# HGRN and gated linear attention: copy the last token tiles first, round the next weights after the first unit's exponentials

## The reference

```python
def chunk_gla(q, k, v, g):
    # S_t = diag(exp(g_t)) S_(t-1) + k_t v_t^T ; o_t = S_t^T q_t, a decay per key channel
    G = jnp.cumsum(g, axis=-2)
    def step(S, inp):
        q_c, k_c, v_c, G_c, qd_c, kd_c, gl_c = inp
        rel = jnp.exp(jnp.where(incl, G_c[..., :, None, :] - G_c[..., None, :, :], -jnp.inf))
        a = jnp.einsum('bhcd,bhsd,bhcsd->bhcs', q_c, k_c, rel)
        o_c = jnp.einsum('bhcd,bhde->bhce', qd_c, S) + jnp.einsum('bhcs,bhse->bhce', a, v_c)
        ...

def hgrn2(x, w_in, lb, norm_w, w_out):
    q, f, i, r = jnp.split(x @ w_in, 4, axis=-1)     # gates from f, values from i
    ...
    o = chunk_gla(q, k, i, log_f)                    # 8 heads of 128; GLA: 4 heads
    o = gated_rms_norm(o, r, norm_w)
    return o @ w_out
```

## Time and profile before

| | |
|---|---|
| median of 3 runs | 2507.51 us (2505.46 to 2508.47) |
| profiled execution | 2507.87 us, of which the span of the trace is 2506.2 |
| PE busy | 2430.0 us, 97% of the span |
| DVE, ACT, POOL busy | 71%, 47%, 4% |
| mean granted TensorE clock | 0.985 of full speed |
| HGRN, last token product to last score in place | 1474 to 1523 us |
| GLA, the same | 1828 to 1859 us |

### The profile page before, as it was taken

One profiled execution on the slowest core, in us unless ns is written; L12 is line 12 of the kernel. 1 busy time (PEld: TensorE's weight loads), 2 busy tenths in 40 slices (PEclk: granted clock), 3 DMA queues, 4 the chain that ended last, 5 costly groups with the idle time before them and its releaser, 6 DMA issues.

```text
span 2506.2 us, 47998 instructions
## 1 busy us (share of the span) xinstructions
PE 2430.0 (97%) x18262; PEld 2248.3 (90%) x18262; DVE 1767.6 (71%) x2908; ACT 1187.6 (47%) x1849; POOL 108.3 (4%) x161
## 2 busy tenths in 40 slices
PE   9999999999999999989999999999989999989998
PEld 6867977788898999988999998999989999978998
DVE  5878799988847866685665867666467657676665
ACT  5554522223645444465444545444545446465444
POOL 2221000000000000000300000000000000000000
PEclk9999999999999999999999999999999999999999
DMA  7423355554424555322555532555424554322554
GB/s 301 143 101 135 110 184 188 181 183 157 177 93 144 195 178 164 118 93 68 180 185 190 162 107 68 192 181 181 160 67 162 185 174 161 102 86 76 195 176 132
DMA packets 119709, 378.21 MB, mean 151 GB/s; under 512 B 11655, under 2 KB 29063, under 8 KB 119184
## 3 DMA queue, kind: packets, MB, share of 16 engines
q1 hardware_dynamic: 107040, 328.62, 39.3%
q0 software_dynamic: 12528, 47.62, 5.6%
HBM read 375.15 MB, written 1.05 MB: 150 GB/s over the span
## 4 chain that ended last, share of the span: by engine, by line
PE 83%; DVE 10%; ACT 4%; issue 2%; DMA 1%; SPq 0%; DVEq 0%; ACTq 0%
PE gb L643 22%; PE gb L644 21%; PE gb L645 21%; DVE w_lo L612 2%; PE mb L2996 2%; PE mb L751 1%; ACT w_hi L604 1%; PE mb L644 1%; PE mb L643 1%; PE mb L645 1%; PE gb L2977 1%; DMA X<-in_x 1%; DVE W L2731 1%; DVE R L1620 1%; DVE W L1620 1%
## 5 line engine op out<-in xcount | busy, mean ns | idle before, releaser
L643 PE MATMUL gb<-Xs,w_hi 128*128 128x256 f32 (+1 forms) x3454 | 1053.6, 305 | 17.8 <-DVE w_lo L612 5.8
L645 PE MATMUL gb<-Xs,w_lo 128*128 128x256 f32 (+1 forms) x3454 | 1036.4, 300 | 0.0
L644 PE MATMUL gb<-Xs,w_hi 128*128 128x256 f32 (+1 forms) x3368 | 1007.7, 299 | 0.0
L604 ACT ACTIVATE w_hi<-raw 128x1024 fp32r<-128x1024 f32 x586 | 614.9, 1057 | 733.6 <-PE gb L645 681.5
L612 DVE TENSOR_TENSOR w_lo<-raw,w_hi 128x1024 fp32r<-128x1024 f32 x586 | 709.6, 1222 | 217.6 <-ACT w_hi L604 211.1
L643 PEld LDWEIGHTS gb<-Xs,w_hi 128*128 128x128 f32 x3454 | 655.5, 190 | 67.6 <-issue 25.0
L645 PEld LDWEIGHTS gb<-Xs,w_lo 128*128 128x128 f32 x3454 | 655.6, 190 | 26.8
L644 PEld LDWEIGHTS gb<-Xs,w_hi 128*128 128x128 f32 x3368 | 639.9, 190 | 23.6 <-issue 1.7
L644 PE MATMUL gb<-Fs,w_hi 128*128 128x256 f32 (+1 forms) x966 | 277.2, 287 | 0.0
L643 PE MATMUL gb<-Fs,w_hi 128*128 128x256 f32 (+1 forms) x880 | 247.7, 281 | 0.0
L645 PE MATMUL gb<-Fs,w_lo 128*128 128x256 f32 (+1 forms) x880 | 246.1, 280 | 0.0
(11 more groups left out here) (459 smaller groups left out, 3315.7 us busy)
## 6 DMA issues: line engine op xcount, KB each, us to landing
raw<-in_up SPq DMA_DIRECT2D x264, 512.0 KB, 3.3
raw<-in_down SPq DMA_DIRECT2D x96, 512.0 KB, 3.7
R<-in_mod_later POOLq DMA_DIRECT2D x80, 512.0 KB, 3.9
raw<-in_gdn_in SPq DMA_DIRECT2D x64, 512.0 KB, 3.3
raw<-in_down SPq DMA_DIRECT2D x48, 384.0 KB, 3.9
raw<-in_hgrn_in SPq DMA_DIRECT2D x32, 512.0 KB, 4.4
raw<-in_ev_in SPq DMA_DIRECT2D x24, 512.0 KB, 5.2
raw<-in_gla_in SPq DMA_DIRECT2D x24, 512.0 KB, 3.9
```

The lines of the kernel that those rows point to most:

```text
L604: nc.scalar.activation(hi, raw[:, slot, 0:hi.shape[1]] if len(hi.shape) == 3 else like(raw[:, slot], hi), ACT.Identity).then_inc(*hi_ready ...
L643: nc.tensor.matmul(to, weight_block(w_slot, 0, k), x_hi, start=start, stop=False)
L644: nc.tensor.matmul(to, weight_block(w_slot, 0, k), x_lo, start=False, stop=False)
L645: return nc.tensor.matmul(to, weight_block(w_slot, 1, k), x_hi, start=False, stop=stop)
```

## The change

A new function `act_last_tokens` takes the place of `act_keep_tokens` in the second pass of token tiles, in HGRN and in GLA. It rounds two tiles (0' and 1') after the first pair as before, makes the first two copies, and then makes the other two copies with no rounding ahead of them. The roundings of 2' and 3' are in `act_gla_core`, behind the exponentials of unit 0. DVE makes three rests instead of four in that pass, and the rest of 2' behind the last `place`, ahead of the normalisation. The loops of one trip around the pass are gone on ACT and DVE. PE, SP and POOL have the same instructions as before.

```diff
--- before.py
+++ after.py
@@ -3041,6 +3041,9 @@
                     nc.scalar.activation(span_exp[u % 2][:, :, 4 * b:4 * b + 4, :],
                                          gb[:, 2 * b:2 * b + 2, :].rearrange("p c (t l i) -> p l (c t) i", t=2, l=2), ACT.Exp,
                                          scale=1.0 / 16 if z.name == "gla" else 1.0).then_inc(*spans_exp.inc())
+                if u == 0:
+                    for _ in range(2):
+                        split_hi(act, ahead["act"].next())
             level_rows.due("act", 4)
 
             def square(c):
@@ -3099,9 +3102,19 @@
                 if u + 1 < len(z.units):
                     rows(u + 1)
                 place(u)
+            dve_tile(dve)
             head_out.due("dve", 4)
             gn_dve_out(dve, z.items, z.parts)
 
+
+        def act_last_tokens(act, to):
+
+            act_tile(act, 2, wait=True)
+            for u in range(BANKS):
+                if u >= 2:
+                    act.wait_ge(*gemm_out.due("act"))
+                gemm_taken.due("act")
+                nc.scalar.activation(to[u // 2][:, u % 2:u % 2 + 1, :], gb[:, u, 0:T].unsqueeze(1), ACT.Identity).then_inc(*gemm_taken.inc())
 
         def pe_hgrn(pe, ready):
             z = hgrn_
@@ -3134,7 +3147,7 @@
             act.wait_ge(*gate_turned.due("act"))
             for b in range(4):
                 nc.scalar.activation(Xs[:, 2 * b:2 * b + 2, T:2 * T], score_banks[b].rearrange("p (a c) -> p a c", a=2), ACT.Identity).then_inc(*gate_hi.inc())
-            act_keep_tokens(act, 4, T, lambda i: z.v[:, :, bass.ds((i + 2) * T, T)])
+            act_last_tokens(act, [z.v[:, :, 2 * T:3 * T], z.v[:, :, 3 * T:4 * T]])
             act_gla_core(act, z)
 
         def dve_hgrn(dve):
@@ -3184,7 +3197,9 @@
                 last = nc.vector.tensor_tensor(Xs[:, KC + 2 * b:KC + 2 * b + 2, T:2 * T], score_banks[b].rearrange("p (a c) -> p a c", a=2),
                                                Xs[:, rows, T:2 * T], ALU.subtract)
             last.then_inc(*gate_lo.inc())
-            dve_pass(dve, 4)
+            dve_tile(dve, 3)
+            gemm_out.due("dve", 4)
+            gemm_taken.due("dve", 4)
             dve_gla_core(dve, z)
 
 
```

## The result

| | before | after |
|---|---|---|
| median of the runs of one occasion | 2504.86 us (20 runs, 2499.84 to 2511.44) | 2500.90 us (20 runs, 2496.50 to 2506.22) |
| profiled execution, its span | 2507.87, 2506.2 us | 2500.57, 2498.9 us |
| mean granted clock | 0.985 | 0.987 |

The ratio is 0.9980, with a 95% interval of 0.9973 to 0.9987: the changed kernel is 5.0 us faster by the ratio (3.3 to 6.8), and 4.0 by the two medians. The forecast was 4.6 us less (2502.9 against 2507.51, 0.9982) and most likely no difference of over 0.2% (0.54). Two executions on record, one of before at 7695.36 us and the profiled one of long_fill at 11646.79 us, stand apart from all others and are used in no ratio and no reading.

The account below looks back on a forecast made before the run. PE was taken as the bound, busy 2430.0 of 2506.2 us, so only its idle waits pay. From the median 2507.51, less 3.82 for the copies and 0.8 for the clock, other terms 0: 2502.9 us, range 2500.4 to 2506.0.

Parts of the forecast that it names:

- Term 1: PE's wait before exponents(0) in HGRN and GLA: copies start 1.91 us earlier in each, 3.82 us gained in all.
- Term 2: ACT between exponentials of units 0 and 1: moved roundings cost PE 0; 1.59 us idle left in HGRN, GLA 0.19 late.
- Term 3: DVE ahead of the normalisation L1391: the moved rest of 2' takes 1.16 of 2.36 us idle, cost 0.
- Term 4: SP's load of tile 6' into slot 2: issued later but landing 9 us before ACT's rounding, cost 0.
- Term 5: PE's clock at the two 2.72 us gaps: a quarter of a fall at each, 0.8 us gained, ends 0 and 3.0.
- The class: Whole kernel, borders at 0.2% (5.0 us) from no change: within 0.54, faster 0.43, slower 0.03.
- B: Clock falls usual at one of the two gaps are gone: 2500.7 to 2502.1 us, middle 2501.3; chance 0.43.
- C: Half the gain: the wait returns in HGRN or GLA as another one, 2505.6 us; chance 0.05.
- D: ACT loads tables twice per layer around the moved roundings, 3.7 us late together, 2507.4 us, no gain; chance 0.01.
- E: Moved work not covered: roundings delay unit 1's exponentials, the rest of 2' delays normalisation, 2509.8 us; chance 0.03.
- F: Clock falls three times in HGRN's units of 64-column scores, 3.0 us each, 2512.7 us, slower; chance 0.03.

Follow-up runs that it names:

- long_fill: long_gap with six unused 512-column products on PE in each of the two gaps: 2511.45 us against 2506.51 for the kernel before, ratio 1.0014.
- hgrn_only: The whole change in HGRN alone, GLA as in the kernel before: 2503.56 us against 2506.87, ratio 0.9989.
- gla_only: The whole change in GLA alone, HGRN as in the kernel before: 2503.42 us against 2506.87, ratio 0.9986.
- dve_only: Kernel before with only DVE's part (three rests in the pass, the rest of 2' behind the last place), ACT unchanged: 2508.40 us against 2506.87, ratio 1.0008.
- long_gap: Kernel before with the two roundings ahead of the last copies each made twice in both mixers: 2513.44 us against 2505.66, ratio 1.0033.
- long_fill_look: The same kernel as long_fill, run once more for its profile: 2508.27 us (one run) against 2508.28 for the kernel before.
- fill_short: Kernel before with three unused 512-column products on PE in each 2.72 us gap: 2506.86 us against 2506.51, ratio 1.0004.
- hi_before_exp: Changed kernel with the two roundings behind the copies but ahead of unit 0's exponentials: 2502.74 us against 2506.87 for the kernel before, ratio 0.9983.

## Why the prediction was right, and where it failed

**Term 1, the copies go ahead: right.** 2 x 1.91 were forecast and 2 x 1.97 measured, and the gap is 0.75 instead of 0.81. HGRN's core is 1.94 shorter, so what follows moves along whole; hgrn_only and gla_only show each alone.

**Term 2, the roundings on ACT at 0: right.** 1.61 us remain in HGRN. In GLA the second exponentials start directly behind the roundings and PE doesn't wait for them: exponents(2) has no idle time ahead of it. Counted from exponents(0) they start 0.09 us later than before, where 0.19 was forecast.

**Term 3, the rest of 2' at 0: right.** 1.22 us in DVE's idle time, 1.23 left (forecast 1.2), and dve_only shows the cores unchanged.

**Term 4, the load of 6' at 0: right by the profile.** The rounding of 6' stands here in the timeline of ACT in the kernel after:

```profile
1539.53 1.04 ACT L604 ACTIVATE Rr<-raw 128x1024 fp32r<-128x1024 f32 x1
```

It starts 62.23 us behind PE's last token product (1477.30), and before it was 64.16 (1537.84 less 1473.68): 1.93 earlier, as all the rest. SP issues the load of 6' at 1526.14, the DMA engines are busy for the next two rows (the last two numbers are their share and GB/s) and idle in the third, so it is there by about 1530, 9.5 us ahead of the rounding (forecast 9):

```profile
1526.00:1528.00 2.00, 2.00 (x13) 1.74 (x12) 0.75 (x1) 0.72 (x2) 0.00 (x0) 1.00 0.46 117
1528.00:1530.00 2.00, 2.00 (x11) 1.55 (x10) 0.75 (x1) 1.70 (x3) 0.00 (x0) 1.00 0.36 145
1530.00:1532.00 2.00, 2.00 (x11) 1.42 (x10) 1.35 (x2) 1.70 (x4) 0.00 (x0) 1.00 0.00 0
```

No run took this step alone.

**Term 5, the clock at 0.8: its size is not settled, and its reason was wrong.** The gains of the change (4.0 to 5.0 on the first occasion, 4.8 to 4.9 on the second) leave 0 to 1 us beside the waits' 3.9, and the estimate from the mean granted clocks is 2.2 us (0.2 to 4.2); 0.8 is inside both. The prediction placed the falls at the gaps of 2.72 us; no profile of any kernel has one there, in 8 gaps of 2.72. They come at 4.89, and behind the wait of 1.17. In the two profiled executions the fall made 3.15 of 7.3 us, near the 3.0 of the prediction's estimate of one fall. That one of the two had it is the luck of the moment at which scores(0) came, by the raster above.

The Trainium skill's "TensorE: Matmul & The Clock Gate", section "What's actually happening", was quoted as a rule by which less idle time can only help. long_gap against long_fill_look agrees (half clock behind 4.89 us of idle time, full clock with PE busy in it); the median of fill_short, 0.04% above before, shows nothing of it. Its section "A second HAM failure mode: psum-queue depth-cycling" describes short, frequent idle times between groups of products by which the clock falls and rises again; here a single wait of 1.17 us was enough, so the case is like it in the shortness and not in the frequency.

**The class: this is the step that failed.** The prediction held 0.2%, 5.0 us, to be what a measurement can tell from no change. It gave no reason for this number, and from it put the likeliest case, a gain of 4.6 us, on the side of no difference, with 0.54. The measured ratio had an interval of 0.07% on each side, 1.7 us, and 4.6 us is 2.6 times that. The gain was forecast to within 0.6 us of what came, by the ratio or by the medians; the border was wrong, not the sum. A second part is the reference: 2507.51 is a median of three, and executions of this kernel lie between 2499.84 and 2511.44, so a median of three can be 2 or 3 us off. That alone moved the forecast time from 2500.3 (2504.86 less 4.6) to 2502.9, against 2500.90 measured, which is only 0.5 above the low end of the range.

**The rivals.** B (the clock gives more, 2501.3) has the time, and by luck: the 2.65 us of the reference put 2500.90 on its side of the border. Its mechanism, a usual fall at one of the two gaps, is in none of the 8 gaps of 2.72; a share of the clock by another way, the moment of scores(0), is not excluded. C is refuted by both gaps being 0.75; D by the missing table load; E by hi_before_exp too, in which the roundings are in the worse place and cost 0.5 us; F by HGRN's core, which has no stretch at half clock.

## What to carry to other kernels

When two things wait in an in-order queue, put first what releases the bounding engine, and look for independent work on that engine for what is left of the wait: here reordering the copies gave about 4 us, and PE's own scores put into the wait gave 2.6 us more of the cores' length. Give the size of a gain as the forecast, and take the border of "no difference" from the spread and number of runs: with 20 runs that spread over 0.5%, 0.1% could be told. Compare stage lengths between fixed points of two traces before reading anything from their spans, since one fall of the clock in one of two profiles (3.15 us) is nearly as large as the effect.

## What the runs showed of the hardware

- Behind idle times of PE of 2.72 us the granted clock stayed full in 8 of 8 places; behind 4.89 us it was 0.50 in 2 of 2; behind 4.9 us in which PE made filler products it was full in 2 of 2.
- A wait of only 1.17 us was followed by 6.83 us at 0.50 in GLA in 7 of 12 profiles, at the products of 64 columns. One such fall costs 3.15 us. Making PE busy in the gap ahead (long_fill_look) didn't prevent it. The moment of scores(0) against the execution's own changes of the clock separates the 7 from the 5, and with the wait filled or cut to 0.21 us none of 3 fell, at moments at which all with the wait did.
- Executions of one unchanged kernel on one core lie 11.6 us (0.46%) apart.
